# Dense projections as three products of high and low parts, and the experts' gate applied to closed sums

## The chip, the cores and the metric

One core of a Trainium2 chip. The metric is the device time of one execution in microseconds, median of several runs. Engines: TensorE (PE, its weight loads PEld), VectorE (DVE), ScalarE (ACT), GpSimd (POOL), and SyncE (SP), whose queue issues the loads of weights.

## The reference

256 tokens of width 1024 go through three blocks, all in fp32. Each projection below is a product with a 1024-deep weight matrix.

```
block A: h = modulate(x);  x += g * gla_mixer(h);        h = modulate(x);  x += g * peer(h)
block B: k, v = shared_kv; x += g * swa(h @ w_q, k, v);  h = modulate(x);  x += g * peer(h)
peer:    q = h @ w_q (2048 wide); top-k over product keys; gelu(h . u_e) * softmax, summed over v_e
block C: proj = u @ w_in  ->  retention q, k, v, g; latents c_q, c_kv, k_pe; two gates
         h += g * ((sigmoid(gr) * ret + sigmoid(gm) * mla) @ w_out)
         h += g * sum_e gate[t, e] * (silu(t @ w1[e]) * (t @ w3[e])) @ w2[e]        (32 experts)
modulation: silu(c) @ mod_w, 160 vectors of 128 outputs; c is one row
```

## The kernel before, in words

Weights come as *slots* of 128x1024 fp32 (512 KB), one after the other from one array `stream`, into a ring of four buffers (`ring`, `RING = 4`). SP issues the loads in program order; a load waits on `ring_free`, which PE raises with the first matmul of each slot, so slot i is fetched when PE starts slot i-3. Between the loads stand those of the *modulation vectors* (`mod_load`): POOL multiplies such a slot with the conditioning vector and halves it three times (`mod_pool`: a product of 128x1024 and three sums of 512, 256 and 128 columns), into two buffers in turn, and PE closes eight of them with one column product each (`mods_pe`). The lists `at` in the program of SP say behind which slot each vector is loaded; a vector's load waits until POOL has made the one two before it, and all that SP has behind it waits too. The vectors are split in segments: `MODS_GLA` 16 to 56, `MODS_SWA` 88 to 104, `MODS_MIX` 136 to 160, and `MODS_DOWN` in the two phases of PEER in which values are summed.

*Dense projections* (`project`, `project_tokens`, L657 to L695) are fp32 matmuls straight from the ring. `project` does one slot: eight matmuls of 128 rows by 256 tokens, which the trace shows as two records each. `project_tokens` does the values, whose outputs are 512 wide. ACT copies each finished tile out of one of four PSUM banks (`copy_act`).

*PEER and the experts* already use three products. ACT copies half a slot (128x512) rounded to fp32r as its high part; DVE or POOL subtracts it from the original for the low part; PE multiplies high by high, high by low and low by high (`up_pe` with POOL's low parts, L2285; `down_pe` and the experts with DVE's, L1992 and L2236). Four half-slot buffers `w_parts` (`HALVES = 4`) hold the parts. The activations are split once (`parts_dve`, 128x2048) into `h_parts`.

*A norm* is a sum of squares on PE, a root on ACT, one Newton step on DVE into `rs`, eight scalings on DVE (`scale_dve`, L1621: `xT` by the gain by `rs`, all in SBUF) and eight shifts on ACT.

*The experts* (`moe_pe`, `moe_act`, `moe_dve`): router product, gate on DVE, then PE transposes the gate and spreads it over the partitions for all 32 experts (L1138, L1146, 32 matmuls, 16 tiles copied by ACT); only then does the first expert's `up` start. For each expert four slots of `up` (L1164), silu on ACT, the product of the two halves and the product with the spread gate on DVE (L2242, L2245), its two parts, and two slots of `down` (L1182), summed over all experts in banks 4 to 7.

## Time and profile before

| | |
|---|---|
| median of 3 runs | 3304.9 us (3303.24 to 3307.88) |
| the profiled execution | 3311.35 us, of it the span 3309.6 us |
| stages of dense projections (us of the span) | 42 to 143, 236 to 294, 1194 to 1255, 1359 to 1417, 2322 to 2526 |
| PEER, first and second | 309 to 1179, 1427 to 2297 |
| router, gate and its spreading | 2696 to 2741 |
| experts | 2741 to 3289 |

A stretch's times are read from the timeline and the windows of the trace; a wait shows as idle time before an instruction, with what ended it in brackets.

### The profile page before, as it was taken

How to read it: one execution, taken by the hardware profiler on the slowest of the kernel's cores; microseconds unless marked ns; L12 is line 12 of the kernel's file. 1: busy time of each engine (PE TensorE's matmuls, PEld its weight loads, DVE VectorE, ACT ScalarE, POOL GpSimd, SP SyncE). 2: the span in 40 equal slices, each digit the busy share in tenths (PEclk: the TensorE clock that was granted, in tenths of full speed). 3: DMA queues.
4: the chain of work that ended last, by engine and by line, in shares of the span. 5: the costliest groups of instructions: out<-in, count | busy, mean ns of one | idle time of the engine just before them, and what ended most of it. 6: DMA issues, size and time to landing. Idle time of an engine off the chain costs nothing.

```text
span 3309.6 us, 56035 instructions
## 1 busy us (share of the span) xinstructions
PE 3078.3 (93%) x18286; PEld 2726.7 (82%) x18286; DVE 1702.8 (51%) x2944; ACT 1666.8 (50%) x3149; POOL 1528.7 (46%) x1220
## 2 busy tenths in 40 slices
PE   8989999987999987999899699999999989999998
PEld 7679999976778866889899677877678779999997
DVE  6633370047888835173400878886301425555555
ACT  2123777788455533167677965555113224555554
POOL 3957998875444443178888644442551000000000
PEclk8979999999999997999999999999999979999999
DMA  6535554521766642345455056664664224555554
GB/s 246 195 133 181 171 171 165 182 78 57 254 228 226 231 141 89 132 140 179 157 179 176 0 184 241 234 222 139 210 208 142 91 81 154 187 186 184 184 185 132
DMA packets 153450, 552.42 MB, mean 167 GB/s; under 512 B 16896, under 2 KB 19712, under 8 KB 153232
## 3 DMA queue, kind: packets, MB, share of 16 engines
q1 hardware_dynamic: 151136, 547.42, 48.7%
q10 hardware_dynamic: 2224, 3.87, 0.4%
q8 instruction: 48, 0.79, 0.1%
q14 instruction: 42, 0.34, 0.0%
HBM read 550.17 MB, written 1.05 MB: 167 GB/s over the span
## 4 chain that ended last, share of the span: by engine, by line
PE 69%; ACT 9%; issue 8%; POOL 7%; DVE 4%; DMA 2%; ACTq 0%; DVEq 0%; POOLq 0%; SPq 0%; PEldq 0%
PE bank L901 19%; PE bank L875 16%; PE bank L1164 11%; PE bank L668 10%; PE bank L1182 5%; ACT hT L1352 5%; POOL w_parts L2285 4%; ACT hT L1348 2%; POOL arena L2317 1%; POOL arena L2319 1%; PE bank L687 1%; DMA ring<-stream 1%; PE bank L1146 1%; DMA arena<-stream 1%; PE bank L630 1%
## 5 line engine op out<-in xcount | busy, mean ns | idle before, releaser
L2285 POOL TENSOR_TENSOR w_parts<-ring,w_parts 128x512 fp32r<-128x512 f32 x512 | 687.2, 1368 | 193.6 <-ACT w_parts L1312 188.8
L875 PE MATMUL bank<-h_parts,w_parts 128*128 128x256 f32 x6144 | 747.5, 284 | 25.1 <-POOL w_parts L2285 23.1
L875 PEld LDWEIGHTS bank<-h_parts,w_parts 128*128 128x128 f32 x6144 | 743.2, 193 | 29.8 <-POOL w_parts L2285 26.8
L1312 ACT ACTIVATE w_parts<-ring 128x512 fp32r<-128x512 f32 x512 | 321.6, 630 | 205.6 <-PE bank L875 201.6
L668 PE MATMUL bank<-hT,ring 128*128 128x256 f32 x1584 | 361.8, 391 | 40.2 <-ACT hT L1245 32.4
L2236 DVE TENSOR_TENSOR w_parts<-ring,w_parts 128x512 fp32r<-128x512 f32 x384 | 265.3, 692 | 244.8 <-ACT w_parts L1505 236.9
L668 PEld LDWEIGHTS bank<-hT,ring 128*128 128x128 f32 x1584 | 308.4, 196 | 92.7 <-issue 33.6
L1164 PEld LDWEIGHTS bank<-h_parts,w_parts 128*128 128x128 f32 x3072 | 374.9, 193 | 5.6 <-issue 3.3
L1164 PE MATMUL bank<-h_parts,w_parts 128*128 128x256 f32 x3072 | 375.8, 284 | 2.6 <-DVE w_parts L2236 2.6
L1505 ACT ACTIVATE w_parts<-ring 128x512 fp32r<-128x512 f32 x384 | 242.2, 632 | 267.7 <-PE bank L1164 174.7
L901 PE MATMUL bank<-h_parts,a_parts 128*128 128x512 f32 x1536 | 366.2, 394 | 6.1 <-DVE a_parts L1995 6.1
L901 PE MATMUL bank<-w_parts,a_parts 128*128 128x512 f32 x1536 | 369.7, 396 | 0.4 <-DVE a_parts L1995 0.3
L901 PEld LDWEIGHTS bank<-h_parts,a_parts 128*128 128x128 f32 x1536 | 284.5, 188 | 81.2 <-DVE a_parts L1995 23.2
L901 PEld LDWEIGHTS bank<-w_parts,a_parts 128*128 128x128 f32 x1536 | 285.9, 190 | 59.2 <-DVE a_parts L1995 1.1
L1250 ACT ACTIVATE arena<-bank 128x256 f32<-128x256 f32 (+2 forms) x222 | 95.1, 428 | 428.2 <-PE bank L668 301.7
L1371 ACT ACTIVATE a_parts<-arena 128x256 fp32r (+1 forms) x256 | 107.1, 418 | 363.1 <-PE bank L901 361.3
L2317 POOL TENSOR_TENSOR arena<-arena,cact 128x1024 f32<-128x1024 f32 x80 | 161.2, 2015 | 261.2 <-DMA arena<-stream 261.1
L1995 DVE TENSOR_TENSOR a_parts<-arena,a_parts 128x256 fp32r<-128x256 f32 x256 | 167.5, 654 | 116.2 <-ACT a_parts L1371 115.9
L849 PE MATMUL bank<-hT,h_parts 128*128 128x128 f32 x1024 | 145.9, 295 | 68.9 <-ACT hT L1352 67.2
L849 PEld LDWEIGHTS bank<-hT,h_parts 128*128 128x128 f32 x1024 | 129.1, 202 | 85.6 <-ACT hT L1352 85.5
L668 PE MATMUL bank<-arena,ring 128*128 128x256 f32 x768 | 175.2, 388 | 8.2 <-DVE arena L1833 6.6
L1182 PE MATMUL bank<-w_parts,a_parts 128*128 128x512 f32 x768 | 180.3, 390 | 2.0 <-DVE a_parts L2251 2.0
(317 smaller groups left out, 4086.2 us busy)
## 6 DMA issues: line engine op xcount, KB each, us to landing
ring<-stream SPq DMA_DIRECT2D x786, 512.0 KB, 3.3
arena<-stream SPq DMA_DIRECT2D x192, 512.0 KB, 4.3
hT<-stream SPq DMA_DIRECT2D x32, 512.0 KB, 4.4
mean<-stream SPq DMA_DIRECT2D x32, 512.0 KB, 4.5
arena<-consts ACTq DMA_DIRECT2D x1, 1536.0 KB, 6.8
xT<-xin ACTq DMA_DIRECT2D x1, 1024.0 KB, 10.6
out<-hT SPq DMA_DIRECT2D x4, 256.0 KB, 2.2
arena<-subk ACTq DMA_DIRECT2D x2, 128.0 KB, 2.1
```

Of the source, the lines that this page charges most:

```text
L668: mm = pe.matmul(t[:, 0:T], w[:, q * P:(q + 1) * P], src[:, q, :], start=(q == 0), stop=(q == n - 1))
L849: mm = pe.matmul(bank[4 + k][:, (s % 4) * P:(s % 4 + 1) * P], hot2[:, s, :].bitcast(F32), hot1[:, s, :], start=True, stop=True)
L875: mm = pe.matmul(bank[k][:, 0:T], w[:, wp, ws], h_parts[:, hp, 4 * j + q, :], start=(j == 0 and q == 0 and i == 0), stop=(j == 1 and q == ...
L901: mm = pe.matmul(bank[4 + 2 * a + e][:, :], a_parts[:, k % 2, ap, a * P:(a + 1) * P], w[:, wp, :], start=False, stop=False, skip_group_che ...
L1164: mm = pe.matmul(bank[2 * e_par + m][:, f * T:(f + 1) * T], w[:, wp, q * P:(q + 1) * P], h_parts[:, hp, 4 * j + q, :], start=(j == 0 and q ...
L1182: mm = pe.matmul(bank[4 + 2 * a + e][:, :], a_parts[:, ap, f, a * P:(a + 1) * P], w[:, wp, :], start=(start and f == 0 and i == 0), stop=( ...
L1312: act.activation(w_parts[half % HALVES][:, 0, :], ring[slot_][:, j * 512:(j + 1) * 512], ACT.Copy).then_inc(sem(f"{n}_high"), 1)
L1505: act.activation(w_parts[half % HALVES][:, 0, :], ring[s][:, j * 512:(j + 1) * 512], ACT.Copy).then_inc(sem("e_high"), 1)
L1995: dve.tensor_tensor(a_parts[:, k % 2, 1, :], W[:, bass.ds(it * 16 + k, 1), :].rearrange("p i t -> p (i t)"), a_parts[:, k % 2, 0, :].bitca ...
L2236: dve.tensor_tensor(w[:, 1, :], ring[moe_slot(k)[0]][:, j * 512:(j + 1) * 512], w[:, 0, :].bitcast(F32), ALU.subtract).then_inc(sem("e_low ...
L2285: pool.tensor_tensor(w[:, 1, :], ring[(base + k) % RING][:, j * 512:(j + 1) * 512], w[:, 0, :].bitcast(F32), ALU.subtract).then_inc(sem(f" ...
L2317: pool.tensor_tensor(b3, b3, c_b, ALU.mult).then_inc(sem("mod_step"), 1)
```

## The change

Ninety-two slots of the dense projections (14 of each PEER's 16 query slots; 2 of 4 key slots, 4 value slots and 6 of 8 query slots of the window attention; all but the first 2 of the mixer's input) become three products. ACT makes each half slot's high part, DVE its low part, two slots ahead of PE in program order, through the same four `w_parts`. The first two slots behind each norm stay fp32 while DVE splits the activations, now in two pieces (`parts_dve`). DVE's other work in these stages is put between the low parts (`behind`), ACT's between the high parts (`evict_split`). In the experts the gate no longer multiplies `hid`: each expert's `down` is a closed sum in banks 4 to 7, which DVE multiplies by the gate and adds to `B.y`; the gate's transposes, products and copies go. The first four slots' low parts come from POOL (`moe_pool`), while DVE makes the gate. Eight modulation vectors (152 to 160) move from the mixer to the experts (`MODS_MOE`), and the lists `at` change: three vectors are loaded inside the first sixteen slots, the others spaced for shorter slots. The norm's result goes to PSUM (`root`, in bank 6), from where `scale_dve` reads it. The rotation of the window attention's keys and the scaling of `S.h` are moved behind later slots.

```diff
-MODS_MIX = (136, 160)
+MODS_MIX = (136, 152)
+MODS_MOE = (152, 160)
+        root = bank[6][:, T:2 * T]
-            at = [gla + 1 + 3 * i // 2 for i in range(16)] + [gla + 27] * 8
-            at += [q0 - 4 + 5 * i // 4 for i in range(16)]
+            at = [8, 10, 14, gla + 1] + [gla + 2 + 3 * i // 2 for i in range(14)] + [gla + 27] * 6
+            at += [gla + 28] * 2 + [min(q0 - 4 + 5 * i // 3, q0 + 15) for i in range(14)]
-            at = [kv + i for i in range(10)] + [MO["swa_out"][0] + 2] * 4 + ...
+            at = [kv + 3 * i // 2 for i in range(10)] + [MO["swa_out"][0] + 2] * 4 + ...
-            loads_with_mods(mix, MO["mix_out"][1], MODS_MIX, MODS_MIX[0], [mix + 2 * i - i // 8 for i in range(24)])
+            loads_with_mods(mix, MO["mix_out"][1], MODS_MIX, MODS_MIX[0], [mix + 5 * i // 2 for i in range(16)])
...
+        def project_split(pe, name, k, tile, parts=None):
+            t = open_tile(tile)
+            pe.wait_ge(free_sem(tile), freed(tile) - 1)
+            for j in range(2):
+                ...
+                w = split_parts(name, k, j)
+                pe.wait_ge(sem("x_low"), split_half(name, k, j) + 1)
+                for q in range(4):
+                    for i, (wp, hp) in enumerate(((0, 0), (0, 1), (1, 0))):
+                        mm = pe.matmul(t[:, 0:T], w[:, wp, q * P:(q + 1) * P], h_parts[:, hp, 4 * j + q, :], ...)
...
+        def split_high(act, name, k, j):
+            half = split_half(name, k, j)
+            act.wait_ge(landed_sem(name, k), landed_at(name, k))
+            if half >= HALVES:
+                act.wait_ge(sem("x_passed"), half - HALVES + 2)
+            act.activation(split_parts(name, k, j)[:, 0, :], slot(name, k)[:, j * 512:(j + 1) * 512], ACT.Copy)...
+        def evict_split(act, work):
+            for i, (_, evict) in enumerate(work):
+                high = work[i + 2][0] if i + 2 < len(work) and work[i + 2][0] in SPLIT else None
+                if high is not None:
+                    split_high(act, *high, 0)
+                evict()
+                if high is not None:
+                    split_high(act, *high, 1)
...
+            for i, step in enumerate(rotation("q", M.q)):
+                behind[("ret_k", 2 + i)] = step
+            for i, step in enumerate(rotation("k", M.k)):
+                behind[("ret_v", 2 + i)] = step
...
+            def add_up(e, k, expert, step, summed):
+                dve.wait_ge(sem("e_half_free"), step(2 * k + e + HALVES - 1))
+                dve.wait_ge(sem("e_summed"), summed + 2 * (e + 1))
+                for a in range(TT):
+                    n = 2 * a + e
+                    dve.scalar_tensor_tensor(B.y[:, n, :], bank[4 + n][:, :], E.gate[:, a, expert], B.y[:, n, :],
+                                             ALU.mult, ALU.add).then_inc(sem("e_summed"), 1)
```

The first place is DVE in the mixer's input projections, around the rotation of the retention queries (`arena<-arena` of 1024 columns). Before:

```order
L1636 SCALAR_TENSOR_TENSOR xT<-xT,vec,rs 128x256
L1639 SCALAR_TENSOR_TENSOR hT<-xT,gain,arena 128x256
L2082 TENSOR_TENSOR arena<-arena 128x1024
L2084 TENSOR_TENSOR arena<-arena 128x1024
L2086 TENSOR_TENSOR arena<-arena 128x4x256
L2088 TENSOR_TENSOR arena<-arena 128x4x256
L2090 TENSOR_TENSOR arena<-arena 128x4x256
L2092 TENSOR_TENSOR arena<-arena 128x4x256
```

The same place of the changed kernel; `w_parts<-ring,w_parts` are the low parts, two for each slot:

```order
L1737 SCALAR_TENSOR_TENSOR hT<-xT,gain,arena 128x256
L1746 CAST h_parts<-hT 128x1024
L1748 TENSOR_TENSOR h_parts<-hT,h_parts 128x1024
L1746 CAST h_parts<-hT 128x1024
L1748 TENSOR_TENSOR h_parts<-hT,h_parts 128x1024
L1756 TENSOR_TENSOR w_parts<-ring,w_parts 128x512 x18
L2218 TENSOR_TENSOR arena<-arena 128x1024
L1756 TENSOR_TENSOR w_parts<-ring,w_parts 128x512 x2
L2222 TENSOR_TENSOR arena<-arena 128x1024
L1756 TENSOR_TENSOR w_parts<-ring,w_parts 128x512 x2
L2222 TENSOR_TENSOR arena<-arena 128x4x256
```

The six steps of the rotation stood together; now one stands behind each pair of low parts, and the pair after it waits for it.

The second place is PE from the router product (`128x36`) to the first experts. Before, with the gate's transposes and its 32 spreading products:

```order
L1129 MATMUL bank<-ring,hT 128x36 x16
L1138 MATMUL bank<-cst,arena 32x128 x2
L1146 MATMUL bank<-arena,cst 128x256 x32
L1164 MATMUL bank<-h_parts,w_parts 128x256 x192
```

The same place of the changed kernel:

```order
L747 MATMUL bank<-arena,ring 128x256 x8
L649 MATMUL bank<-hT,cst 128x256 x3
L1204 MATMUL bank<-ring,hT 128x36 x16
L1223 MATMUL bank<-h_parts,w_parts 128x256 x192
L1244 MATMUL bank<-w_parts,a_parts 128x512 x24
```

The gate's matmuls are gone, and the products of the first two experts stand right behind the router's.

## Rows read from the trace of the kernel before

**Rows 1.** Page, part 1: busy us, share of the span, instructions

```profile
PE 3078.3 (93%) x18286; PEld 2726.7 (82%) x18286; DVE 1702.8 (51%) x2944; ACT 1666.8 (50%) x3149; POOL 1528.7 (46%) x1220
```

**Rows 2.** Windows of six stretches: length, busy, PEclk, DMA share, GB/s

```profile
236.00:294.00 58.00, 57.45 (x259) 50.35 (x260) 6.15 (x9) 8.96 (x23) 43.44 (x40) 0.96 0.70 236
1194.00:1256.00 62.00, 60.74 (x237) 46.51 (x238) 14.98 (x29) 12.30 (x30) 43.91 (x40) 0.96 0.62 219
...
2322.00:2527.00 205.00, 200.47 (x868) 162.39 (x869) 33.15 (x42) 35.62 (x70) 112.90 (x96) 0.97 0.58 199
2691.00:2741.00 50.00, 35.67 (x100) 28.43 (x100) 14.51 (x49) 18.35 (x35) 0.00 (x0) 0.54 0.03 11
2741.00:3283.00 542.00, 540.07 (x3816) 510.00 (x3815) 322.04 (x479) 273.89 (x446) 0.00 (x0) 1.00 0.56 183
```

**Rows 3.** The chain, whole span: start, us, what

```profile
2380.88 27.47 PE bank L687 x64
...
2678.08 3.45 PE bank L668 x16
...
2788.65 11.51 PE bank L1164 x96
2800.17 5.47 PE bank L1182 x24
```

**Rows 4.** Timeline from 2690 us: start, us, engine, line, operation, idle before

```profile
2696.51 7.01 PE L1129 MATMUL bank<-ring,hT 128*128 128x36 f32 x32 [5.42 <-ACT hT L1245]
...
2700.45 2.29 DVE L1647 TENSOR_TENSOR h_parts<-hT,h_parts 128x2048 fp32r<-128x2048 f32 x1
...
2710.44 27.67 PE L1146 MATMUL bank<-arena,cst 32*128 32x256 f32 x64 [0.52 <-ACT arena L1250]
...
2740.72 19.49 PE L1164 MATMUL bank<-h_parts,w_parts 128*128 128x256 f32 x142 [2.61 <-DVE w_parts L2236]
```

**Rows 5.** Page, part 5: shapes, count, busy us, mean ns, idle before

```profile
L2285 POOL TENSOR_TENSOR w_parts<-ring,w_parts 128x512 fp32r<-128x512 f32 x512 | 687.2, 1368 | 193.6 <-ACT w_parts L1312 188.8
...
L1312 ACT ACTIVATE w_parts<-ring 128x512 fp32r<-128x512 f32 x512 | 321.6, 630 | 205.6 <-PE bank L875 201.6
...
L2236 DVE TENSOR_TENSOR w_parts<-ring,w_parts 128x512 fp32r<-128x512 f32 x384 | 265.3, 692 | 244.8 <-ACT w_parts L1505 236.9
```

**Rows 6.** Timeline of POOL from 286 us: the last vector of this stage

```profile
286.18 1.90 POOL L2317 TENSOR_TENSOR arena<-arena,cact 128x1024 f32<-128x1024 f32 x1
...
290.31 0.46 POOL L2329 TENSOR_TENSOR arena<-arena 128x128 f32<-128x128 f32 x1
```

**Rows 7.** Timeline of DVE from 2020 us

```profile
2021.52 1.28 DVE L1992 TENSOR_TENSOR w_parts<-arena,w_parts 128x512 fp32r<-128x512 f32 x2
...
2024.22 2.99 DVE L1992 TENSOR_TENSOR h_parts<-arena,h_parts 128x512 fp32r<-128x512 f32 x2
```

**Rows 8.** Timeline of POOL over the same stretch

```profile
2024.71 1.96 POOL L2317 TENSOR_TENSOR mean<-mean,cact 128x1024 f32<-128x1024 f32 x1 [4.93 <-DMA mean<-stream]
...
2029.40 0.71 POOL L2329 TENSOR_TENSOR hT<-mean 128x128 f32<-128x128 f32 x1 [0.16 <-POOL mean L2321]
```

**Rows 9.** Groups of DVE by shape: a PSUM operand, POOL at work beside it

```profile
L1960 DVE TENSOR_TENSOR h_parts<-bank,mean 128x512 fp32r<-128x512 f32 x128 | 87.2, 684 | 0.1
```

**Rows 10.** Timeline of DVE, first rotation of the mixer

```profile
2353.87 1.23 DVE L2082 TENSOR_TENSOR arena<-arena 128x1024 f32<-128x1024 f32 x1 [26.08 <-ACT arena L1250]
...
2356.38 2.80 DVE L2086 TENSOR_TENSOR arena<-arena 128x1024 f32<-128x1024 f32 x1
```

**Rows 11.** Timeline of PE at the end of the first queries

```profile
295.70 1.93 PE L696 MATMUL bank<-cst,arena 128*128 128x1 f32 x16
```

**Rows 12.** Timeline of PE behind the values of the mixer

```profile
2414.09 6.11 PE L668 MATMUL bank<-hT,ring 128*128 128x256 f32 x18 [3.84 <-DMA ring<-stream]
```

**Rows 13.** Timeline of DVE, the first norm scaled

```profile
41.38 9.23 DVE L1621 SCALAR_TENSOR_TENSOR hT<-xT,gain,rs 128x256 f32<-128x256 f32 x8
```

**Rows 14.** Timeline from 2690 us, the last norm scaled

```profile
2695.34 3.26 DVE L1621 SCALAR_TENSOR_TENSOR hT<-xT,gain,rs 128x256 f32<-128x256 f32 x8
```

More of the change, by code:

```diff
@@ L78 @@
 MODS_SWA = (88, 104)
-MODS_MIX = (136, 160)
+MODS_MIX = (136, 152)
+MODS_MOE = (152, 160)
+SPLIT = [(name, k) for name, first, last in
+         (("peer0_q", 2, 16), ("kv_k", 2, 4), ("kv_v", 0, 4), ("swa_q", 2, 8), ("peer1_q", 2, 16), ("ret_q", 2, 8),
+          ("ret_k", 0, 8), ("ret_v", 0, 8), ("mla_cq", 0, 3), ("mla_ckv", 0, 2), ("mla_kpe", 0, 1), ("ret_g", 0, 8),
+          ("gate_r", 0, 8), ("gate_m", 0, 8)) for k in range(first, last)]
 STREAM = [
@@ L1159, in up @@
                             half = 2 * (k + 2 * m + f) + j
-                            pe.wait_ge(sem("e_low"), step(half + 1))
+                            pe.wait_ge(sem(lows), step(half + 1))
                             w = w_parts[half % HALVES]
@@ L1170, in up, with down @@
                             mm.then_inc(sem("e_half_free"), 1)
-            def down(k, step, hidden, start=False, stop=False):
+            def down(k, step, hidden, summed):
                 pe.wait_ge(sem("e_hlow"), hidden)
@@ L1295, in peer_act @@
             n = f"p{l}"
-            for j in range(16):
-                copy_act(act, R.q[:, j, :], f"{n}_q{j}")
+            evict_split(act, evictions(act, f"peer{l}_q", f"{n}_q", lambda j: R.q[:, j, :], 16))
             for a in range(TT):
@@ new lines, in roots @@
+            def roots():
+                act.wait_ge(sem("norm_ln"), signalled("norm_ln"))
+                for r in (rs[:, :], G2.r2):
+                    act.activation(r, r, ACT.Exp, scale=-0.5).then_inc(sem("norm_root"), 1)
+            work = evictions(act, "ret_q", "r_q", lambda c: M.q[:, c, :], 8)
+            work += evictions(act, "ret_k", "r_k", lambda c: M.k[:, c, :], 8)
+            work += evictions_tokens(act, "ret_v", "r_v", M.v, 2)
+            work += evictions(act, "mla_cq", "m_cq", lambda c: M.cq[:, c, :], 3)
@@ new lines, in mix_act @@
+            work += evictions(act, "mla_ckv", "m_ckv", lambda c: M.ckv[:, c, :], 2)
+            work += [(("mla_kpe", 0), latent)]
+            work += evictions(act, "ret_g", "r_g", lambda c: M.g[:, c, :], 8, ACT.Silu)
+            work += evictions(act, "gate_r", "r_gate", lambda c: M.gr[:, c, :], 8, ACT.Sigmoid)
+            work += evictions(act, "gate_m", "m_gate", lambda c: M.gm[:, c, :], 8, ACT.Sigmoid)
+            at = work.index(next(of for of in work if of[0] == ("gate_r", 0)))
+            first, second = work[at][1], work[at + 1][1]
@@ L1456, in mix_act @@
+            work[at] = (work[at][0], logs)
+            work[at + 1] = (work[at + 1][0], lambda: [roots(), first(), second()])
+            evict_split(act, work)
             act.wait_ge(full_sem("r_s3"), filled("r_s3"))
@@ L1843, in peer_dve @@
             parts_dve(dve, n, f"{l}b")
+            for j in range(2, 16):
+                split_lows(dve, f"peer{l}_q", j)
             if l == 0:
```

426 lines of the change are left out of this document (257 added, 169 removed).

## The prediction

> **What bounds the kernel now.** I read the page first: PE is busy for 93% of the span [rows 1]. The chain shows how it is busy: long unbroken pieces of matmuls, one after the other [rows 3]. Then the windows by stage show where it is not at full rate: the stretch from the router to the experts has a mean granted clock of 0.54, while the experts run at 1.00 with 540 of 542 us busy [rows 2]. So time is won by shorter PE work, and lost wherever PE waits for an engine that feeds it. In the dense stages before the change nothing feeds PE but the queue, and DVE is nearly idle (33 of 205 us in the mixer's), but POOL is not: 43 of 58 us, 44 of 62 us, 113 of 205 us [rows 2].
>
> **The products.** At full clock an fp32 slot takes 3.45 us, a value slot 27.47/8 = 3.43 us; four slots of the experts' three-product form take 11.51 us, 2.88 each, and two of its 512-wide form 5.47, 2.74 each [rows 3]. That is 0.57 us less for 80 slots (45.8 us) and 0.70 less for 12 (8.4 us): **54.2 us** in all, if every half slot is ready. By stage: 14 first queries 8.0, window attention 7.4 (8 and 4 slots), second queries 8.0, mixer 30.8 (44 and 8).
>
> The Trainium skill (FP8 and Floating Point Precision, TensorE Precision Notes) says that true fp32 takes four passes. Three in place of four would make a slot 2.59 us and the sum 79 us. The rows show 2.88, and the sum goes by them.
>
> **Who feeds it.** For each slot ACT adds two high parts of 0.63 us [rows 5] to its one copy, well under 2.88. DVE adds two low parts of 0.69 us [rows 5]; the pair takes 1.28 us. But beside a working POOL the pair takes 2.99 us [rows 7, 8]: the product of a vector on POOL started 0.5 us after it. POOL loses too: one vector lasts 5.4 us there [rows 8] against 4.6 us beside an idle DVE [rows 6]. An operation that reads PSUM and one tensor of SBUF keeps 0.68 us for 512 columns, with POOL subtracting and summing beside it in that phase [rows 9]. This is the price that decides the dense stages, since POOL works in three of the four. The Trainium skill (GPSIMD Engine Reference, Key points) says that GpSimd shares its SBUF interfaces with VectorE and contends with instructions of two SBUF inputs; the low parts are that kind, and the trace agrees.
>
> **First queries, +2.5 us of 8.0.** POOL has its last vector at 290.77 us [rows 6], and PE closes the group of columns at 295.70 to 297.6 [rows 11]. With 14 shorter slots PE would be done 8 us sooner, about 286. But nine vectors are left after 236 us by the new list (before: ten), each 5.4 us and not 4.6: the first lands at 244.5, and 9 x 5.4 us end at 293, or, at 4.6 us each with the last ones held by their late loads, at 288. PE waits for the last group. I take 292 and a little lost clock: 2.5 us won; bounds 0 and 8. DVE's 2.99 us for a pair is also just above 2.88, worth 1.5 us on 14 slots, hidden by that same wait.
>
> **Window attention, +2 of 7.4.** Ten vectors are now spaced 1.5 slots, 4.3 us, for a POOL that wants 5.4 each, so POOL works throughout. DVE has six slots of pairs with eight scalings, the split of `S.h`, then six pairs with four rotations of keys. Beside POOL the last part alone is 6 x 2.99 + 4 x about 2.3 = 27 us for PE's 6 x 2.88 + 2 = 19 us. With the lead of the buffers (about 2 us) that takes away 5 to 6 us. Bounds: -1 and 7.4.
>
> **Second queries, +8.0.** POOL has nothing there, so the pair costs 1.28 us of 2.88. Bounds 7 and 8.
>
> **Mixer, +23.** 30.8 us of shorter products, and 3.8 us of a stall that goes: behind the values PE waits 3.84 us for a slot [rows 12] because SP stood at a vector's load that waited for POOL, and POOL for PE's columns; the new spacing (every 2.5 slots) brings the ninth vector's load behind that point. Against it: six slots of the keys and six of the values have a rotation step each. One is 1.23 us alone and 2.80 beside POOL [rows 10]. A slot's DVE work is then 1.28 + 1.25 = 2.5 us free and about 5.3 contended; POOL works 5.4 us in each 2.5 slots. With PE slowed to t a slot, t = 2.5 + 2.7 x (5.4/2.5)/t gives t = 4.0, 1.1 us too much, six times, less 2 us of lead: 5 us for each rotation, 10 for both. The roots of the two latents put four ACT table changes and copies behind each other, 1.5 us. 30.8 + 3.8 - 10 - 1.5 = 23. Bounds: 14 and 34.6. Without POOL's contention the rotations fit in 2.88 and cost nothing.
>
> **Start of the experts, +35.** Before, the router's product ends at 2703.5 and the first `up` starts at 2740.7, 37.2 us later, of which 27.7 are the spreading products at low clock [rows 4]. Afterwards `up` needs the parts of the activations (2702.7 before [rows 4]) and POOL's first low part: ACT has slots 0 and 1 rounded by 2702, and POOL needs 1.37 us for each half [rows 5] against 1.44 us of PE. Both are ready near 2704. DVE's gate is not needed until the first closed sum is added, but ACT's third high part stands behind the first exponential, which hangs on DVE; PE has two slots of work by then. For contention between POOL's low parts and DVE's split and gate I take off 2 us. Bounds 31 and 37.
>
> **Experts, -2.5.** DVE is busy 322 of 542 us [rows 2]. For each of 32 experts it loses one operation of 0.69 us and gains four of 512 columns from PSUM, 0.68 each [rows 9]: 322 + 32 x 2.0 = 387 us. The additions stand before `hidden_low`, which then comes 2.3 us later; counted from the start of `up`, the fourth slot's last high part can follow at 5.75 us, so the low part of `hid` is made near 9.3, and `down` starts at 11.5. It fits, by 1.5 to 2 us. Eight vectors on POOL make three or four pairs slow each; I give each 0.3 us. Bounds 0 and -15.
>
> **First norm, 0.** The scaling takes 9.23 us beside POOL [rows 13] and 3.26 without it [rows 14]; from PSUM it should take 3.3 to 3.9. That is 5.5 us, against three more loads and POOL's work inside the first 40 us, where DVE is as busy: 2 to 9 us. I take 0; bounds -4 and +5. At the end the four copies of ACT give way to two of DVE's additions, and a group of columns moves there: 0.
>
> **Sum.** 2.5 + 2 + 8 + 23 + 35 - 2.5 + 0 = **68 us**. The profiled execution's span becomes 3309.6 - 68 = 3241.6. Its own time, 3311.35, is 6.4 above the median of the runs, so I predict 3304.9 - 68 = **3237 us**.
>
> **The rivals.** *No contention (0.22).* The low parts' lead covers everything: 54.2 + 3.8 + 37 = 95, 3210 us. For it: PEER's value phase has DVE at its low parts and POOL at vectors, and PE hardly waits there. Against: that phase has eight half buffers, this one four, and POOL pauses there as long as it works. *Dense stages bound by DVE and POOL (0.20).* First queries 0, window attention -1, mixer 14, experts' start 33, experts -8, second queries 7: 45 us, 3260 us. *The change does not do it (0.05).* Interleaved with evictions the products keep PE at about 3.4 us a slot; only the experts' start and the stall are won: 3266 us. *Slower (0.03).* The additions hold `hidden_low` past the end of `up`. One late expert costs what it is late, 32 times; the 68 us and more are gone from 2.2 us each, which needs DVE to be 3.7 to 4.2 us later than counted. At 3 us each it is 3333 us. For it: five operations in a row before `hidden_low`; against: they read PSUM. *The forecast* has 0.50, its own range 3222 to 3252.
>
> Leaving out the slower case, the outer part of the last two and the best of the first, the range is 3207 to 3265. What a measurement of this kernel tells from no change is 0.2%, 6.6 us: faster 0.95, within it 0.02, slower 0.03.
>
> **What would show it.** In the second queries 2.9 us a slot and no wait for DVE. In the mixer's keys and values waits of PE for `w_parts` from DVE behind each rotation step, and pairs near 3 us wherever POOL works. Before the second group of columns in the first queries a wait of PE, ended by POOL. The first `up` within 3 us of the router's end. In the experts 16.98 us for each. I am wrong if pairs of low parts stay near 1.3 us beside POOL, if POOL's vectors end early, or if experts show a wait before `down`.

## The result and the profile after

The changed kernel runs in 3251.1 us (median of 4, 3245.69 to 3253.32), the kernel before in 3306.39 us (median of 4, 3303.24 to 3314.96). The ratio is 0.9826, 95% interval 0.9803 to 0.985, and 55.3 us are gained by the medians. Of the two profiled executions the spans are 3309.6 and 3243.9 us. One execution of e6 below took 5883.66 us where its three others took 3262.7 to 3268.6; nothing here explains it, and the ratios leave it out.

The page of the changed kernel, part 1 (busy us, share of the span, instructions), to be held against [rows 1], and the groups by line of the new slots:

```profile
PE 2985.8 (92%) x18908; PEld 2694.4 (83%) x18908; DVE 1982.0 (61%) x3234; ACT 1762.6 (54%) x3309; POOL 1583.7 (49%) x1229
...
L695 PE MATMUL bank<-h_parts,w_parts 128*128 128x256 f32 x1920 | 240.6, 287 | 15.2 <-DVE w_parts L1756 13.2 <-DVE arena L2162 1.9
...
L719 PE MATMUL bank<-w_parts,h_parts 128*128 128x512 f32 x144 | 34.9, 395 | 6.3 <-DVE w_parts L1756 6.2
...
L1756 DVE TENSOR_TENSOR w_parts<-ring,w_parts 128x512 fp32r<-128x512 f32 x184 | 196.5, 1100 | 60.8 <-ACT w_parts L1297 59.5 <-DVE arena L2222 0.3
```

PE has 92 us less to do, and it waits 21.5 us before the split products (15.2 and 6.3), 19.4 of them ended by DVE's low parts (L1756), whose mean is 1100 ns where the experts' of the same shape cost 692 [rows 5]. That is where the dense slots lose. The windows of the changed kernel (length, busy of PE, PEld, DVE, ACT, POOL, PEclk, DMA share, GB/s), each from the first matmul of a stage to that of the next:

```profile
226.90:290.90 64.00, 56.73 (x404) 54.92 (x405) 44.08 (x39) 25.60 (x51) 47.26 (x36) 0.90 0.60 206
1187.70:1254.70 67.00, 56.62 (x313) 50.35 (x314) 55.38 (x58) 25.81 (x52) 53.41 (x39) 0.91 0.57 204
1254.70:1293.60 38.90, 21.86 (x81) 14.43 (x80) 36.96 (x65) 13.66 (x56) 19.23 (x18) 0.62 0.12 41
1359.20:1409.30 50.10, 49.35 (x368) 47.84 (x369) 24.95 (x38) 26.27 (x51) 0.00 (x0) 0.96 0.52 168
2312.00:2491.20 179.20, 168.24 (x1230) 156.89 (x1230) 143.30 (x147) 95.99 (x171) 91.06 (x64) 0.99 0.61 205
2661.80:2670.20 8.40, 7.02 (x33) 6.91 (x33) 8.23 (x14) 4.73 (x11) 5.15 (x3) 0.50 0.20 62
2670.20:3223.60 553.40, 547.44 (x3843) 515.83 (x3843) 396.03 (x596) 273.78 (x447) 52.04 (x39) 0.99 0.57 187
```

They are the first queries, the projections of the window attention, its rotations up to the attention, the second queries, the mixer's dense part, router to first `up`, and the experts. With POOL at 0.00 (second queries) PE is busy for 49.4 of 50.1 us. With POOL at work beside DVE it is busy for 57 of 64 and of 67 us, and the granted clock is 0.90 and 0.91 instead of the 0.97 and 0.96 of the kernel before in these two stages.

The same boundaries in all kernels, read from each timeline, are this table (us; the columns e1 to e12 are experiments below, and the experiments without a column have the stages that matter in their text):

| stage | before | after | e1 | e2 | e3 | e4 | e9 | e10 | e12 |
|---|---|---|---|---|---|---|---|---|---|
| start to chunk loop | 144.8 | 148.6 | 146.6 | 147.2 | 140.1 | 137.5 | 148.1 | 150.6 | 148.5 |
| chunk loop | 50.6 | 36.1 | 51.4 | 51.5 | 46.9 | 37.8 | 36.1 | 36.1 | 36.1 |
| first queries | 61.2 | 64.0 | 61.6 | 64.8 | 64.7 | 54.6 | 65.3 | 64.3 | 61.2 |
| window: projections | 60.3 | 67.0 | 59.4 | 59.7 | 67.4 | 51.9 | 54.3 | 66.9 | 52.8 |
| window: rotations | 38.5 | 38.9 | 38.3 | 37.8 | 38.8 | 30.3 | 35.4 | 38.8 | 35.4 |
| window: attention | 22.5 | 22.7 | 23.0 | 23.4 | 22.8 | 22.5 | 26.3 | 22.8 | 26.3 |
| second queries | 58.3 | 50.1 | 58.6 | 49.9 | 50.2 | 50.0 | 50.2 | 50.1 | 50.3 |
| mixer, dense | 204.2 | 179.2 | 195.8 | 178.8 | 180.4 | 166.4 | 181.8 | 168.9 | 168.9 |
| mixer, behind it | 170.3 | 170.6 | 171.0 | 170.8 | 170.3 | 169.9 | 171.3 | 174.5 | 174.6 |
| router to first `up` | 44.2 | 8.4 | 8.4 | 8.4 | 8.4 | 8.4 | 8.4 | 8.4 | 8.4 |
| experts | 548.1 | 553.4 | 553.9 | 553.5 | 550.2 | 549.7 | 553.9 | 553.4 | 553.5 |

### The profile page after: what moved, and what is told of

Read it like the earlier page. It is cut to its first block, busy times and chain, and to the rows that moved or that the text cites. A ratio compares the mean times of both kernels' runs of the same rounds, so it can differ in the third digit from the quotient of the medians.

```text
span 3243.9 us, 57950 instructions
## 1 busy us (share of the span) xinstructions
PE 2985.8 (92%) x18908; PEld 2694.4 (83%) x18908; DVE 1982.0 (61%) x3234; ACT 1762.6 (54%) x3309; POOL 1583.7 (49%) x1229
## 4 chain that ended last, share of the span: by engine, by line
PE 66%; issue 9%; ACT 9%; POOL 8%; DVE 6%; DMA 1%; ACTq 0%; POOLq 0%; DVEq 0%; SPq 0%
PE bank L978 20%; PE bank L952 15%; PE bank L1223 11%; PE bank L747 6%; PE bank L1244 5%; ACT hT L1444 5%; POOL w_parts L2460 5%; PE bank L695 3%; ACT hT L1440 2%; POOL arena L2504 1%; DVE w_parts L1756 1%; POOL arena L2506 1%; POOL arena L2508 1%; DMA arena<-stream 1%; DMA ring<-stream 0%
## 5 line engine op out<-in xcount | busy, mean ns | idle before, releaser
L952 PE MATMUL bank<-h_parts,w_parts 128*128 128x256 f32 x6144 | 745.6, 284 | 25.3 <-POOL w_parts L2460 23.3
L952 PEld LDWEIGHTS bank<-h_parts,w_parts 128*128 128x128 f32 x6144 | 741.3, 193 | 29.7 <-POOL w_parts L2460 27.2
L1223 PEld LDWEIGHTS bank<-h_parts,w_parts 128*128 128x128 f32 x3072 | 374.2, 193 | 3.8 <-DVE arena L2322 1.5
L1223 PE MATMUL bank<-h_parts,w_parts 128*128 128x256 f32 x3072 | 375.1, 284 | 1.4 <-DVE arena L2322 1.4
L2391 DVE TENSOR_TENSOR w_parts<-ring,w_parts 128x512 fp32r<-128x512 f32 x376 | 271.1, 732 | 149.0 <-ACT w_parts L1596 145.7
L978 PEld LDWEIGHTS bank<-h_parts,a_parts 128*128 128x128 f32 x1536 | 284.9, 188 | 79.0 <-DVE a_parts L2107 20.8
L978 PEld LDWEIGHTS bank<-w_parts,a_parts 128*128 128x128 f32 x1536 | 286.8, 190 | 60.3 <-DVE a_parts L2107 2.0
L695 PE MATMUL bank<-h_parts,w_parts 128*128 128x256 f32 x1920 | 240.6, 287 | 15.2 <-DVE w_parts L1756 13.2
L695 PEld LDWEIGHTS bank<-h_parts,w_parts 128*128 128x128 f32 x1920 | 236.3, 195 | 18.9 <-issue 14.6
L1756 DVE TENSOR_TENSOR w_parts<-ring,w_parts 128x512 fp32r<-128x512 f32 x184 | 196.5, 1100 | 60.8 <-ACT w_parts L1297 59.5
```

Of the source, the lines that this page charges most:

```text
L695: mm = pe.matmul(t[:, 0:T], w[:, wp, q * P:(q + 1) * P], h_parts[:, hp, 4 * j + q, :], start=(j == 0 and q == 0 and i == 0), stop=(j == 1 ...
L952: mm = pe.matmul(bank[k][:, 0:T], w[:, wp, ws], h_parts[:, hp, 4 * j + q, :], start=(j == 0 and q == 0 and i == 0), stop=(j == 1 and q == ...
L978: mm = pe.matmul(bank[4 + 2 * a + e][:, :], a_parts[:, k % 2, ap, a * P:(a + 1) * P], w[:, wp, :], start=False, stop=False, skip_group_che ...
L1223: mm = pe.matmul(bank[2 * e_par + m][:, f * T:(f + 1) * T], w[:, wp, q * P:(q + 1) * P], h_parts[:, hp, 4 * j + q, :], start=(j == 0 and q ...
L1756: dve.tensor_tensor(w[:, 1, :], slot(name, k)[:, j * 512:(j + 1) * 512], w[:, 0, :].bitcast(F32), ALU.subtract).then_inc(sem("x_low"), 1)
L2391: dve.tensor_tensor(w[:, 1, :], ring[moe_slot(k)[0]][:, j * 512:(j + 1) * 512], w[:, 0, :].bitcast(F32), ALU.subtract).then_inc(sem("e_low ...
```

## The experiments

Each kernel ran beside the kernel before on one chip; the ratio is to that one. Each changes the kernel after, unless it says otherwise.

**e1: no split slots.** Of the 92 slots none is split; the rest stays.

```diff
-SPLIT = [(name, k) for name, first, last in (("peer0_q", 2, 16), ... ("gate_m", 0, 8)) for k in range(first, last)]
+SPLIT = []
...
             for of in order:
-                split_lows(dve, *of)
```

> The changed kernel with all 92 projection slots as fp32 products again: no high and low parts of them, everything else (the order of the mixer, the root in PSUM, the experts' gate on closed sums, the vectors' places) as changed. Theory (the gain is two independent sums): the experts keep their part, router to first up product about 8 us instead of 44; the mixer goes back from 179 to about 201 (the changed order of the latents is still in), the second queries from 50 to 58, the window attention from 67 to about 60, the first queries from 64 to about 61. Time about 3251 + 20 = 3271 us, 0.989 of before. Rival (part of the gain is the higher granted clock in the chunk loop, 0.92 against 0.68 there, and comes from the parts): the chunk loop falls back to 52 us and the time is about 3285.

Measured 3267.88 us, ratio 0.9863 (0.9843 to 0.9884). The table has both parts apart: the experts keep 8.4 us at their start, and the second queries go back by 8.5. The mixer goes back by 16.6 us only, from 179.2 to 195.8, not to 204.2. So 8.4 of its 25.0 us come from the new order (latents ahead of `ret_g`, eight vectors and a group of columns less, the stall gone) and not from the parts. The window of the mixer's dense part in e1 shows PE busy throughout and DVE nearly idle again:

```profile
2331.90:2527.70 195.80, 195.28 (x846) 158.35 (x847) 34.15 (x39) 31.52 (x67) 76.47 (x64) 0.99 0.52 186
```

The first queries and the window's projections become shorter without the split, by 2.4 and 7.6 us. By stages the 92 split slots bring 8.5 + 16.6 - 2.4 - 7.6 = 15.1 us, 0.5% of the time, and by the two ratios 0.4%. The span of e1 holds a slow chunk loop (below) and longer PEER phases too, so the stages are compared and not the spans. The chunk loop is at 51.4 us here, which is the rival's number; e2 shows that it has nothing to do with the split.

**e2: the window attention in fp32.** `kv_k`, `kv_v` and `swa_q` leave `SPLIT`, and DVE scales and rotates as before.

```diff
-         (("peer0_q", 2, 16), ("kv_k", 2, 4), ("kv_v", 0, 4), ("swa_q", 2, 8), ("peer1_q", 2, 16), ("ret_q", 2, 8),
+         (("peer0_q", 2, 16), ("peer1_q", 2, 16), ("ret_q", 2, 8),
...
-            project_tokens_split(pe, "kv_v", "kv_v", 1)
+            project_tokens(pe, "kv_v", hT, "kv_v", 1)
```

> The changed kernel with the twelve split slots of the window attention (kv_k, kv_v, swa_q) as fp32 products again; the other 80 stay split. Theory (VectorE is the bound there: parts, pairs of lows at 2.9 beside the vectors, scalings and rotations together need more than TensorE saves): the stage from the first key product to the first rotation product goes from 66.9 back to about 60, time about 3251 - 6 = 3245 us, 0.9815 of before. Rival (what is lost in the stage is the half clock or a late load, which fp32 products don't cure, or the attention behind it takes the gain back): within 2 us of the changed kernel, 3249 to 3253.

3246.48 us, ratio 0.9801 (0.978 to 0.9821). The projections take 59.7 us: the split there costs 7.3 us. The whole time falls by 4.6 us, less than its own spread of 9, so it is the stage that shows it. Up to 1187 us this kernel is the changed one, instruction for instruction, and so is e7 below. Yet the windows over the chunk loop, of e2 and then of e7, differ by 15.3 us:

```profile
147.20:198.70 51.50, 44.30 (x214) 39.26 (x213) 19.46 (x32) 8.60 (x12) 26.44 (x24) 0.64 0.13 47
```

```profile
148.50:184.70 36.20, 31.59 (x215) 28.49 (x214) 17.96 (x32) 8.60 (x12) 26.52 (x24) 0.88 0.19 65
```

The same instructions ran at a granted clock of 0.64 in one execution and of 0.88 in the other. The kernel before had 0.67 and 50.6 us in its profile. At the same low clock the changed kernel's loop (51.5 us) is thus no shorter than the one before (50.6). The 14.5 us in that row of the table are not a gain that these runs let one credit to the change.

**e3: the first vectors where they were.**

```diff
-            at = [8, 10, 14, gla + 1] + [gla + 2 + 3 * i // 2 for i in range(14)] + [gla + 27] * 6
+            at = [gla + 1 + 3 * i // 2 for i in range(16)] + [gla + 27] * 8
```

> The changed kernel with the loads of the first vectors where they stood before (none behind rows 8, 10 and 14; sixteen from the second gate slot on at 3/2 slots, eight together behind them). Theory (those three vectors on GpSimdE slow VectorE's work on the first modulation vectors, 2.7 to 3.7 us instead of 1.15): the z product comes about 4 us earlier, at 67 to 68 instead of 71.75, and the time is about 3247. Rival (the higher clock of the chunk loop comes from the vectors being gone from it): the chunk loop has vectors again, runs at 0.68 and takes 52 us instead of 38, and the time is about 3260.

3249.15 us, ratio 0.9816 (0.9792 to 0.984): no difference. The z product comes at 63.8 us instead of 71.7, earlier than the foreseen 67 to 68, and the gain is given back 120 us later. Timeline of PE at the end of e3's chunk loop:

```profile
183.11 3.58 PE L775 MATMUL bank<-cst,arena 128*128 128x1 f32 x16 [15.45 <-POOL arena L2516]
```

PE waits 15.45 us for the last vectors of POOL. That is not the rival's slow clock (up to 167 us the loop was granted 1.00) but a wait that the early loads had removed. The kernel before has these loads at the same places and doesn't show the wait: POOL was done at 180.75 us, and the loop at the low clock reached the last columns only at 186.63. At the full clock it would presumably have waited for POOL too, as e3 did, whose loop took 46.9 us and not 36; that was not run.

**e4: POOL's vectors cut short.** Outside the peer stages the product of a vector runs over 128 columns and its first two additions over 32, which leaves out most of their sums; all else runs as before, on other values.

```diff
+            ks, n4, n2 = (slice(0, DC), 512, 256) if it is not None else (slice(0, 1), 32, 32)
-            pool.tensor_tensor(b3, b3, c_b, ALU.mult).then_inc(sem("mod_step"), 1)
+            pool.tensor_tensor(b3[:, ks, :], b3[:, ks, :], c_b[:, ks, :], ALU.mult).then_inc(sem("mod_step"), 1)
...
-            pool.tensor_tensor(buf[:, 0:512], buf[:, 0:512], buf[:, 512:1024], ALU.add).then_inc(sem("mod_step"), 1)
+            pool.tensor_tensor(buf[:, 0:n4], buf[:, 0:n4], buf[:, 512:512 + n4], ALU.add).then_inc(sem("mod_step"), 1)
```

> The changed kernel with GpSimdE's work on the vectors outside the peer stages cut to almost nothing: the product runs over 128 of 1024 columns and the first two additions over 32 (so those modulation vectors are wrong; loads, columns and order stay). Theory (contention: VectorE's pairs of lows take 2.9 us instead of 1.28 only where GpSimdE works on a vector): the mean of the lows falls from 1100 ns to about 700, TensorE's waits for them (15.2 us in the slots, 6.3 in the values) nearly vanish, the window attention takes about 60, the mixer about 168, the first norm is 3 to 5 us shorter; time about 3228 us, 0.976. Rival (VectorE is simply full, or the loads pace it): lows stay over 1000 ns and the time over 3243.

3184.97 us, ratio 0.9622 (0.9593 to 0.965), 66 us under the changed kernel where 23 were expected. The groups by line of e4:

```profile
L695 PE MATMUL bank<-h_parts,w_parts 128*128 128x256 f32 x1920 | 233.2, 284 | 1.0 <-DVE w_parts L1756 1.0
...
L719 PE MATMUL bank<-w_parts,h_parts 128*128 128x512 f32 x144 | 33.3, 390 | 0.0
...
L1756 DVE TENSOR_TENSOR w_parts<-ring,w_parts 128x512 fp32r<-128x512 f32 x184 | 127.6, 701 | 110.5 <-ACT w_parts L1297 109.4 <-DVE arena L2222 0.2
```

The low parts are at 701 ns, and PE's 21 us of waits are 1.0. The windows of the window attention's projections and of the mixer's dense part:

```profile
1168.50:1220.40 51.90, 51.86 (x313) 47.49 (x314) 34.09 (x58) 26.32 (x52) 15.76 (x37) 0.96 0.72 253
...
2269.10:2435.50 166.40, 164.61 (x1230) 156.80 (x1231) 100.41 (x147) 95.75 (x171) 32.48 (x64) 0.99 0.63 220
```

DVE does the same 58 and 147 instructions in 34 and 100 us instead of 55 and 143, and the loads are not slower, so neither the loads nor DVE's own count is the limit. What the expectation missed most is the window attention: it loses 15.1 us to the vectors in its projections and 8.6 in its rotations (38.9 to 30.3), which the kernel before lost too (38.5). By the spans 60 us are gone: besides those two 11.1 before the chunk loop, 9.4 in the first queries, 12.8 in the mixer, 3.7 in the experts and 2.8 behind the chunk loop, while other stretches are 3 us longer. The 3.7 in the experts lie at their end, in a wait and in the clock behind it (see e8). It is a bound and no version.

**e5 and e9: the window's vectors after the rotations.** Five vectors beside the projections, the others from the last rotated query on. In e5 they stand behind the load of row `kv + 15`, in e9 ahead of it:

```diff
-            at = [kv + 3 * i // 2 for i in range(10)] + [MO["swa_out"][0] + 2] * 4 + ...
-            loads_with_mods(kv, MO["peer1_q"][0], MODS_SWA, MODS_SWA[0], at)
+            m = loads_with_mods(kv, kv + 15, MODS_SWA, MODS_SWA[0], [kv + 3 * i for i in range(5)])  # e5: kv + 16
+            sp.wait_ge(sem("w_qr"), 8)
+            for _ in range(9):                                                                       # e5: 8
+                mod_load(MODS_SWA, m)
+                m += 1
+            loads_with_mods(kv + 15, MO["peer1_q"][0], MODS_SWA, m, [kv + 15, kv + 16])              # e5: [kv + 16] * 3
```

> The changed kernel with its split slots kept, but the sixteen vectors of the window attention in other places: five in the projections (instead of ten, with four more behind them beside the rotations), eight only once the eight queries are rotated, three in the output projection. Theory (what costs is the time in which GpSimdE works on a vector beside VectorE's lows and rotations: without that work the projections took 51.9 us instead of 67.0 and the rotations to the attention 30.3 instead of 38.9): projections about 60, rotations about 31, the attention's 22.7 a few us more; time about 3251 - 12 = 3239 us, 0.9795. Rival (the time is only moved: the attention's VectorE work is slowed by as much): projections and rotations shorter, the attention longer by 10 or more, the time at 3248 to 3252.

> As e5_window_spread, but the nine later vectors stand ahead of the load that the first output projection frees (not behind it), and two behind it: five vectors beside the projections, nine from the last rotated query on, two in the output projection. Theory (in e5_window_spread the projections and rotations took 82.9 us instead of 105.9, and all of it and more was lost because SyncE waited for vectors ahead of the weights, 22.4 us of TensorE's wait for a load): no wait for a load in the output projection, 43 instead of 77 us there, the attention at 23 to 27; time about 3251 - 20 = 3231 us, 0.977. Rival (vectors beside the attention slow its VectorE steps as they slowed the rotations): the attention takes over 30 us, time 3240 or more.

e5: 3263.22 us, ratio 0.9874 (0.9858 to 0.9891), slower than the changed kernel by 12 us of the medians. Its projections (52.9 us) and rotations (30.0) won 23 us, its attention stayed at 23.4, and then the output projection took 77.0 us instead of 42.9, with two waits for loads, 22.39 us and 7.82 us. Timelines of e5, POOL and then PE:

```profile
1303.87 1.90 POOL L2508 TENSOR_TENSOR arena<-arena,cact 128x1024 f32<-128x1024 f32 x1 [57.60 <-DMA arena<-stream]
```

```profile
1335.69 4.54 PE L751 MATMUL bank<-arena,ring 128*128 128x256 f32 x12 [22.39 <-DMA ring<-stream]
```

Row `kv + 15` can't be loaded before the output projection's first matmul (1298.4 us). SyncE stood there with the vectors behind it, and then the next weights stood behind the vectors. Neither theory had said that. e9, with nine vectors ahead of that load, has 3236.71 us, ratio 0.979 (0.977 to 0.9809), by the medians 14 us under the changed kernel, by the ratios 12. The output projection is at 42.9 again. The projections gain 12.7 us, the rotations 3.5, and the attention loses 3.6 (22.7 to 26.3): vectors cost there too, but far less than beside the low parts.

**e6 and e10: the mixer's vectors behind its dense part.** All sixteen, two to a load (e6); or eight at one for five slots and eight behind, one to a load (e10). Both have eight more part buffers, and group 18 of the columns (in e6 both groups) stands ahead of `ret_o`.

```diff
-            loads_with_mods(mix, MO["mix_out"][1], MODS_MIX, MODS_MIX[0], [mix + 5 * i // 2 for i in range(16)])
+            loads_with_mods(..., [mix + 52 + i // 2 for i in range(16)])                            # e6
+            loads_with_mods(..., [mix + 5 * i for i in range(8)] + [mix + 50 + i for i in range(8)])  # e10
```

> The changed kernel with the sixteen vectors of the mixer behind its dense part, beside its scores and latents, where GpSimdE did nothing (with their own eight parts more, and their columns ahead of the retention's output projection). Theory: the dense part falls from 179.2 to about 168 (166.4 with the vectors' work cut away), the part behind it stays within 3 of 170.6; time about 3251 - 10 = 3241, 0.980. Rival (the part behind it hangs on VectorE's and ActE's short steps, which the vectors slow): the part behind grows by 8 or more and the time stays at 3249 to 3253.

> The changed kernel with eight of the mixer's vectors in its dense part, one for five slots instead of two, and eight behind it, one for each load (e6_mixer_late had all sixteen behind, two for each load: dense 162.2, the rest 202.1, of which 14.3 us were waits for loads). Theory (the loss there was SyncE's order, not contention): dense part about 169, no waits for loads behind it, the rest 173 to 175; time about 3251 - 7 = 3244 us, 0.981. Rival (GpSimdE beside the mixer's short steps is what costs): the rest at 180 or more, time over 3250.

e6: 3268.49 us, ratio 0.9892 (0.9872 to 0.9911). The dense part is 162.2 us, even under e4's 166.4 since 4 us of columns left it, and the part behind it is 202.1 instead of 170.6. The timeline of PE in e6 has the waits:

```profile
2512.80 4.54 PE L1130 MATMUL bank<-arena,ring 128*128 128x256 f32 x12 [4.58 <-DMA ring<-stream]
2521.60 5.36 PE L1130 MATMUL bank<-arena,ring 128*128 128x256 f32 x12 [4.26 <-DMA ring<-stream]
...
2539.91 5.60 PE L1158 MATMUL bank<-ring,arena 128*128 128x512 f32 x8 [5.49 <-DMA ring<-stream]
...
2550.22 0.82 PE L1167 MATMUL bank<-arena 128*128 128x256 f32 x2 [2.97 <-DVE arena L2162]
...
2560.79 3.57 PE L775 MATMUL bank<-cst,arena 128*128 128x1 f32 x16 [5.09 <-POOL arena L2516]
```

The rival expected the part behind to grow, by contention. Of its 31.5 us 5.1 are the wait for POOL's last vector and 4 the columns that moved there. But 14.3 are loads that queue behind vectors, as in e5: a vector's load waits until POOL has finished the vector two before, about 5 us, and every weight behind it waits along. e10 keeps that spacing wide: no wait for a load behind the dense part, dense 168.9, behind 174.5, and 3244.7 us, ratio 0.9812 (0.9792 to 0.9833). That interval too overlaps the changed kernel's, so it is the stages that show the gain of 6.4 us.

**e7: five mixer slots in fp32.** Keys 3, 5 and 7 and values 3 and 5, whose rotation steps stay.

```diff
+         if (name, k) not in (("ret_k", 3), ("ret_k", 5), ("ret_k", 7), ("ret_v", 3), ("ret_v", 5))]
```

> The changed kernel with five slots of the mixer as fp32 products again (keys 3, 5 and 7, values 3 and 5), those in the stretches where rotation steps stand behind the lows. Theory (VectorE is full there: 9.6 us of TensorE's waits stand in the keys and values): the five slots cost TensorE 3 us and give VectorE five pairs of 2.5 to 3 us, the waits fall under 2; the dense part 179.2 to about 175, time about 3247, 0.982. Rival (the waits come from single pairs that meet a vector, and not from the sum of the work): waits fall by less than 3 us, and the dense part stays at 179 or grows.

3244.02 us, ratio 0.9819 (0.9803 to 0.9836). The dense part is 173.5 us, 5.7 shorter, and PE's waits over 0.5 us in it are two, 1.85 and 0.53 us, where the changed kernel had nine, 9.5 us in all. For this stage leaving five slots unsplit is faster than splitting them, since DVE was full there; the whole time, 7 us less by the medians and 2 by the ratios, doesn't resolve it.

**e8: the last expert's low part first.**

```diff
-            add_up(0, 6 * NE - 2, last, same, 4 * (NE - 2))
             hidden_low(1, NE)
+            add_up(0, 6 * NE - 2, last, same, 4 * (NE - 2))
```

> The changed kernel with the low part of the last expert's hidden values made ahead of the addition of the expert before last, instead of behind its first half. Theory (the wait of 5.08 us before the last down product, 2.05 before the change, is that addition): the wait falls to about 3 and the last products run at full clock again; 2 to 4 us, time about 3248. Rival (the wait is the hidden values themselves): 5 us stay, and no difference.

3251.46 us, ratio 0.9835 (0.9818 to 0.9851), no difference. The wait before the last `down` in the changed kernel and in e8, from the timelines of PE:

```profile
3216.11 7.51 PE L1244 MATMUL bank<-w_parts,a_parts 128*128 128x512 f32 x24 [5.08 <-DVE a_parts L2403]
```

```profile
3225.87 7.53 PE L1244 MATMUL bank<-w_parts,a_parts 128*128 128x512 f32 x24 [5.32 <-DVE arena L2412]
```

Only the name of what ends the wait has changed. The last `down` needs the low part and the banks emptied by the additions, both on DVE, and no `up` of a next expert covers them. The rival's number is right, its reason isn't. Both theories overlooked a third engine. The last of the eight vectors lands just there, beside DVE's last low parts. Timeline of the changed kernel:

```profile
3211.14 1.90 POOL L2504 TENSOR_TENSOR arena<-arena,cact 128x1024 f32<-128x1024 f32 x1 [62.52 <-DMA arena<-stream]
3214.82 1.23 DVE L2403 TENSOR_TENSOR a_parts<-arena,a_parts 128x512 fp32r<-128x512 f32 x1
```

The same place of e4, where the vector is short:

```profile
3157.04 0.68 DVE L2403 TENSOR_TENSOR a_parts<-arena,a_parts 128x512 fp32r<-128x512 f32 x1
3157.77 5.75 PE L1244 MATMUL bank<-w_parts,a_parts 128*128 128x512 f32 x24 [3.36 <-DVE a_parts L2403]
```

The wait is 1.7 us shorter there, and the last products take 5.75 us instead of 7.51. In e8 the vector ran beside the low part itself, which took 2.38 us instead of 0.68, so what the new order could have won wasn't seen.

**e11: first vectors as before, first queries in fp32.** The edit of e3, and `peer0_q` leaves `SPLIT`.

> The changed kernel with the first vectors' loads where they stood before (as e3_old_first) and the fourteen split slots of the first queries as fp32 products again. Theory: the z product comes 8 us earlier (63.8 instead of 71.7) and the first queries take 61.6 instead of 64.0 us; time about 3251 - 9 = 3242 us if the chunk loop is granted the same clock (36 us), 0.9805. Rival (the earlier z product is given back where the gate's vectors then come later): the first queries start no earlier, time 3248 or more.

3249.91 us, ratio 0.9828 (0.9806 to 0.985). First queries 61.7 us, 2.3 less than after. The z product came at 68.4 us and not at 63.8, behind a wait of 4.35 us for ACT. The loop ends with the wait for POOL of e3, 14.44 us, so the rest is given back.

**e12: what gained, together.** e9, e10 and the fp32 first queries, with the changed kernel's first loads.

> The three edits that gained, together: the window attention's vectors as in e9_window_spread2 (3236.7 us), the mixer's as in e10_mixer_half (3244.7), and the first queries as fp32 products with the first vectors' loads as changed (61.7 instead of 64.0 us for that stage in e11_first_fp32). Theory (three stages, nothing shared): the projections to the second queries 1187 to 1346, mixer 169 and 174.5, first queries 62; 3251 - 14 - 6 - 2.5 = 3228 us, 0.9765 of before. Rival (the gains share the waits of a GpSimdE queue that only moved): 3236 or more.

3225.74 us (5 runs, 3217.66 to 3232.91), ratio 0.9759 (0.9735 to 0.9784), by the medians 25 us under the changed kernel, by the ratios 22. Its interval lies below the changed kernel's. The stages add up as in the single kernels. Windows of e12, the window attention's projections and the mixer's dense part:

```profile
1184.90:1237.70 52.80, 52.23 (x313) 47.63 (x314) 40.76 (x58) 26.29 (x52) 24.27 (x19) 0.96 0.57 199
...
2298.10:2467.00 168.90, 163.52 (x1212) 155.07 (x1213) 119.71 (x146) 95.98 (x171) 49.74 (x36) 0.99 0.58 198
```

The same split slots with 24 us of POOL beside them instead of 53 take 52.8 us, 14.2 less.

## Why the prediction was right, and where it was not

**The time.** 3251.1 us lies in the range of 3207 to 3265, 14 above the forecast; 55.3 of 68 us came. Of the profiled difference of 65.7 us, 14.5 are in the chunk loop, a stage in which the prediction had nothing. With both loops at the low clock about 51 would be left, which is also what the seven terms below give (50.4 instead of 68). What the kernel before would take there at the full clock wasn't run; by e3 it would wait for POOL, so the clock alone is probably less than the 14.5. Two terms fell outside their own bounds (the window attention and the first queries), and that the time came within 14 us is in part luck: the profiled loop gained what nobody had counted, and how much of that is in the medians isn't known. In e1 and e2, with the slow loop in their profiles, those executions were also the slowest of theirs, by 13 and 5 us.

**Second queries, +8.0: 8.2.** No POOL, no wait. **Start of the experts, +35: 35.8**, and `up` began 1.4 us after the router's end, ended by DVE's read of the logits. Timeline of the changed kernel:

```profile
2661.80 7.01 PE L1204 MATMUL bank<-ring,hT 128*128 128x36 f32 x32 [5.42 <-ACT hT L1338]
2665.05 6.93 POOL L2492 TENSOR_TENSOR w_parts<-ring,w_parts 128x512 fp32r<-128x512 f32 x4 [212.76 <-ACT w_parts L1596]
...
2670.19 24.86 PE L1223 MATMUL bank<-h_parts,w_parts 128*128 128x256 f32 x192 [1.38 <-DVE arena L2322]
```

**Mixer, +23: 25.0**, but two errors partly cancel. The waits stand where they were foreseen, behind the rotation steps in the keys and values, 9.5 us for the 10 counted. The parts brought 16.6 us, not 20.8, and the new order 8.4 instead of 2.3 (the stall less the latents). Timeline of PE in the values:

```profile
2369.37 11.17 PE L719 MATMUL bank<-w_parts,h_parts 128*128 128x512 f32 x48 [1.75 <-DVE w_parts L1756]
2381.84 2.98 PE L719 MATMUL bank<-w_parts,h_parts 128*128 128x512 f32 x12 [1.30 <-DVE w_parts L1756]
2386.05 3.33 PE L719 MATMUL bank<-w_parts,h_parts 128*128 128x512 f32 x12 [1.23 <-DVE w_parts L1756]
```

The first piece is four slots at 2.79 us; each slot that stands alone between waits takes 2.98 to 3.35, though the granted clock over them was 1.00. Over five key slots and four value slots that is 3 us, which the prediction hadn't counted. The 1.5 us for the latents weren't there: no wait beside their roots was over 0.25 us.

**Window attention, +2: -6.7.** This is the term that failed most, and it missed even its bound of -1. Its mechanism is right: without POOL's work (e4) it is +8.4. The step "That takes away 5 to 6 us" counted 27 us of DVE against 19 of PE in the queries alone. Timeline of PE there:

```profile
1222.29 5.98 PE L695 MATMUL bank<-h_parts,w_parts 128*128 128x256 f32 x48 [1.51 <-DVE w_parts L1756]
...
1233.42 4.62 PE L695 MATMUL bank<-h_parts,w_parts 128*128 128x256 f32 x24 [1.89 <-DVE arena L2162]
1239.24 3.10 PE L695 MATMUL bank<-h_parts,w_parts 128*128 128x256 f32 x24 [1.21 <-DVE w_parts L1756]
1244.68 3.10 PE L695 MATMUL bank<-h_parts,w_parts 128*128 128x256 f32 x24 [2.34 <-DVE w_parts L1756]
1250.12 4.61 PE L695 MATMUL bank<-h_parts,w_parts 128*128 128x256 f32 x24 [2.33 <-DVE w_parts L1756]
```

The waits sum to 9.3 us here and about 10.3 with ACT's two short ones between. Two of the four pieces of 24 matmuls took 4.6 us where the others took 3.10: 3.0 us more, at a granted clock of 0.64 over each of the two and of 1.00 over the others. So the step had 5 to 6 us of loss where there were 10.3 of waits, the first of them already before the first of its six slots, and it had priced a wait at its length alone.

**First queries, +2.5: -2.8.** This term fell outside its bounds of 0 and 8 too. PE waited for POOL's last vectors, as said, 5.36 us. Timelines of POOL (its first vector of the stage, the last step of its last) and of PE:

```profile
237.35 1.90 POOL L2504 TENSOR_TENSOR arena<-arena,cact 128x1024 f32<-128x1024 f32 x1 [11.34 <-DMA arena<-stream]
...
286.58 0.45 POOL L2516 TENSOR_TENSOR arena<-arena 128x128 f32<-128x128 f32 x1
```

```profile
287.09 3.57 PE L775 MATMUL bank<-cst,arena 128*128 128x1 f32 x16 [5.36 <-POOL arena L2516]
```

The stage starts at 226.9 us here and at 236.5 in the kernel before, so the times are to be counted from there. POOL ended 60.1 us after the start, where the prediction had 55.5 (292 less 236.5): its first vector began 10.4 us after the start and not 8.0, and the nine took 49.7 us, not 48.6. The columns behind it took 3.57 us instead of 1.93 [rows 11], again at a lower clock. That is the loss. The products ended later than counted as well (52.8 us after the start, not 49.2), with one wait of 1.87 for DVE, but POOL's end covers that.

**First norm, 0: -3.8** up to the chunk loop. The scaling from PSUM takes 3.22 us instead of 9.23 [rows 13], as foreseen. e3 has it without the early loads and reaches the loop 4.7 us sooner than the kernel before; the early loads then cost 8.5 us, within the 2 to 9 of the prediction. The size is uncertain: the ten kernels with the early loads and whole vectors reach the loop between 146.6 and 151.1 us, and e11, with the old loads, at 142.7 where e3 has 140.1. e3 shows the other half of the edit: later it saves PE a wait of 15 us when the loop runs at full clock.

**Experts, -2.5: -5.3.** The steady part cost nothing, neither the additions nor the vectors: each `down` from the third to the last but one starts 16.98 us after the one before it, as predicted, without a wait. 3.0 us are the longer wait before the last `down` (5.08 instead of 2.05), 1.8 its products at the lower clock, 0.9 a wait before the first. Of the first two, 3.5 us go away in e4, so there it was a vector beside the last low parts (e8). The term was right in size within 3 us and wrong in its cause.

**The rivals.** Contention decides the dense stages (e4), so *no contention* is out. *Dense stages bound by DVE and POOL* (3260) comes nearest in the first queries and the window attention and is wrong in the mixer. By e1 the split is worth 0.4 to 0.5% as built, not nothing. `hidden_low` is never late in the steady state.

## What to carry to other kernels

Before an operand is split on a second engine, look which third engine works beside it. Here 92 split slots gained 0.4 to 0.5% with POOL's vectors beside them, and moving some of those vectors to stages without such work gained as much again (e9 and e10), so their places are part of the same decision. When background loads share a queue with the weights, place them by what stands behind them: a load that can't issue holds every load after it, which cost 30 us in one place (e5) and 14 in another (e6). Where an engine is just overfull, leaving some slots in the old form can be faster than splitting them all (e7, by its stage), and a wait of PE can cost more than its length. A stage that no edit touched can move by 15 us between two profiles, so hold each term against its own stage before the sum is called right.

## What the runs showed of the hardware

- Low parts of the same shape (two operands in SBUF) took 701 ns on average with POOL's vectors cut short and 1100 ns beside them (L1756, 184 of them).
- One unchanged instruction sequence, the chunk loop, was granted 0.64 in one execution (e2) and 0.88 in another (e7) and took 51.5 and 36.2 us. Of eleven profiles of kernels with the changed first loads nine had 36 to 38 us and two 51; the one of before had 50.6. What decides it stayed open, and whether the kernel before falls into the slow form more often wasn't tried.
- After waits of 1.9 and 2.3 us 24 matmuls took 4.62 and 4.61 us, after others of 1.2 and 2.3 us 3.10. The granted clock was 0.64 over each of the two long pieces and 1.00 over each of the two short ones.
- DVE's eight scalings of 128x256 with one operand in PSUM took 3.22 us beside a vector on POOL (after) and 3.22 with the vectors cut short (e4). With all operands in SBUF they took 9.23 us beside POOL [rows 13].
